# The first unit of the first branch's gates, computed between the mLSTM's heads

## The chip, the core and the metric

The kernel runs on one core of a Trainium2 chip. A core has TensorE (PE in the rows; the loading of its stationary operand is PEld), VectorE (DVE), ScalarE (ACT), GpSimd (POOL), and SyncE (SP), which issues nearly all of the weight loads. The metric is the time of one execution on the device in microseconds, and lower is better. A run's number is the median of several executions.

## What is computed

Two blocks follow each other over 256 tokens of 1024 features. The first has two layers with three branches each (an mLSTM, an attention over selected keys, and a differential attention), whose outputs are gated and summed. The second has a retention layer, a convolution and a mixture of eight experts. The change is in the first block, where each layer does this:

```python
def _layer(x, li, ...):
    z = jnp.einsum('btd,dc->btc', _rms(x, norm_mix_g), w_in)
    ...
    h = _mlstm(mq, mk, m_v, m_if[..., :M_HEADS], m_if[..., M_HEADS:])
    y_a = sigmoid(m_o) * _rms(h, m_norm_g)            # branch 0
    y_b = _dsa(sq, sk, sv, iq, ik, i_w)               # branch 1
    y_c = _rms(_diff_attn(dq, dk, dv, lam_val), ...)  # branch 2
    gates = jax.nn.sigmoid(g_pre + b_gate)            # g_pre: 3 x 1024 columns of z
    merged = (gates[:, :, 0] * (y_a @ w_branch[0]) + gates[:, :, 1] * (y_b @ w_branch[1])
              + gates[:, :, 2] * (y_c @ w_branch[2]))
    x = x + merged @ w_out
    ...

def _mlstm(q, k, v, i_pre, f_pre):
    ...
    sw = jnp.exp(dmat - m_t[..., None]) * jnp.einsum('bhntk,bhnsk->bhnts', qc, kc)
    num = jnp.einsum('bhnts,bhnsv->bhntv', sw, vc) + ...
```

## The kernel before

All engines' programs are written out by hand. Each engine runs its instructions in the order in which they are written and waits on semaphores. Nothing is scheduled for it.

**Products in two parts.** A large product is made of three matmuls, high x high, low x high and high x low (`mm3`). For each megabyte of weights (a *unit*) ACT therefore copies a rounded high part out of the ring of six load buffers (`column_highs`, 128x2048), and DVE then subtracts it to make the low part in place (`column_lows`). PE takes a unit only once its low part exists (`take_column` waits for `column_low`). The high part of each unit has a place of its own in memory, listed in `COLUMNS`. Those that matter here: unit g00 (first half of the first 512 gate columns of branch 0) goes to place H, b10 and b11 (the two units of branch 1's weights) go to A2 and D, g01 to E. Place D lies over the columns of z that hold the differential attention's queries and keys. It is free once PE has transposed them, which the kernel says with `place_free["D"]` behind `turn_heads`.

**Order on PE at the place of the change, once in each of the two layers.** The last products of branch 1's attention (`xs,pT`), then `mlstm_weights`: four transposes of the row vectors, then for each of the four heads an *exponents* product, which spreads a row over 128 partitions (its stationary operand has 4 rows, `ybuf,const`), and a *weights* product of queries and keys (`qkbuf`). DVE adds a mask to the exponents, ACT takes their exp, and DVE multiplies it with the weights product (L2413). Then `turn_branch` transposes branch 1's output (8 transposes, `const,yb`), and `turn_heads` the differential queries and keys (16, `const,z`). Then comes g00: 2 matmuls for the bias and 8 x 3 matmuls of 512 columns. Then `mlstm_values` (24 instructions of 129 columns, `v_ext,pbuf`), and `split_branch(1)`, which takes b10 and b11 both before its first matmul (48 matmuls of 512 columns, `ybuf_tmp_high`). The other three units of the gates follow.

**Order on ACT and DVE there.** ACT: exps of the four heads, two copies of branch 1's transposes, four copies of the heads' transposes, the high parts of b11, g01, g02, g03. DVE: the exponents' and weights' evacuations, the two low parts of branch 1, the low parts of b10 and b11, then `mlstm_values`' normalisation, the low part of g01, and the four merges of branch 1.

PSUM has eight banks, handed out in turn by `fill(ALL)`. It skips banks in `open_banks`, which g00's two banks are from its first matmul until g01 is done.

## Time and profile before

| | us |
|---|---|
| median of 3 executions | 2481.36 |
| lowest and highest | 2478.94, 2481.89 |
| span of the profiled execution | 2479.3 |
| PE busy in it | 2449.2 (99%) |
| DVE busy | 1850.2 (75%) |
| ACT busy | 1552.6 (63%) |
| mean granted TensorE clock | 0.994 of full |

The span runs from the first to the last instruction of one execution that the hardware profiler recorded. PE's busy time counts a matmul until its modelled end, so it covers gaps between starts. For the rate of PE, look at the starts of the weight loads (PEld) instead. The place of the change begins at 170.37 us in layer 0 and at 643.50 us in layer 1.

### The profile page before, as it was taken

The numbers are of one execution on the slowest core, as the hardware profiler recorded it, in microseconds if no ns is written. First come the engines' busy times: TensorE is split into PE (matmuls) and PEld (weight loads), VectorE is DVE, ScalarE is ACT, GpSimd is POOL, SyncE is SP. The second block draws the span as 40 slices with busy tenths as digits, with TensorE's granted clock in tenths as the row PEclk, the third lists the DMA queues.
The fourth block names the chain that finished last, engine by engine and source line by source line (L and its number), as shares of the span: only waits on it lengthen the run. The fifth ranks groups of instructions, "written<-read, shape, count | busy, mean of one in ns | idle before, by whom it ended". The sixth has DMA issues, their size and how long they took to land.

```text
span 2479.3 us, 30443 instructions
## 1 busy us (share of the span) xinstructions
PE 2449.2 (99%) x12028; PEld 2044.3 (82%) x12028; DVE 1850.2 (75%) x1856; ACT 1552.6 (63%) x1892; POOL 29.8 (1%) x36
## 2 busy tenths in 40 slices
PE   8999999999999999999999999999999999999998
PEld 8788888897887889978888997888888888788886
DVE  6877744478776546645545578999999999999998
ACT  5675543457565444365444447788878787878886
POOL 0000000000000000010000000000000000000001
PEclk9999999999999999999999998999999999999999
DMA  7444655354435565675555556999999999999996
GB/s 251 152 136 153 221 182 175 132 175 158 135 137 205 202 212 170 207 252 192 198 203 179 162 195 268 392 364 401 376 394 374 398 380 388 390 374 394 372 391 252
DMA packets 183223, 637.96 MB, mean 257 GB/s; under 512 B 11196, under 2 KB 52594, under 8 KB 139914
## 3 DMA queue, kind: packets, MB, share of 16 engines
q1 hardware_dynamic: 179562, 622.87, 68.3%
q0 software_dynamic: 3488, 12.59, 1.3%
q8 instruction: 132, 2.16, 0.3%
q14 instruction: 41, 0.34, 0.0%
HBM read 616.54 MB, written 18.88 MB: 256 GB/s over the span
## 4 chain that ended last, share of the span: by engine, by line
PE 92%; DVE 3%; DMA 2%; ACT 1%; issue 1%; SPq 0%; DVEq 0%; ACTq 0%
PE bank L561 88%; DVE split L2142 2%; PE bank L598 2%; PE bank L903 1%; DMA ring<-in_moe_w_gate 1%; DMA ring<-in_moe_w_up 1%; ACT split L1529 1%; ACT parts L1529 0%; DVE parts L2211 0%; PE bank L1449 0%; DVE oT_high L2156 0%; DVE parts L2122 0%; DMA const<-in_tables 0%; DVE x_resid L2184 0%; DVE tmp L2199 0%
## 5 line engine op out<-in xcount | busy, mean ns | idle before, releaser
L561 PE MATMUL bank<-split,parts 128*128 128x512 f32 (+1 forms) x6432 | 1467.4, 388 | 6.2 <-DVE parts L2211 1.8
L561 PEld LDWEIGHTS bank<-split,parts 128*128 128x128 f32 x6432 | 1186.6, 188 | 253.6 <-issue 15.2
L1529 ACT ACTIVATE split<-ring 128x2048 fp32r<-128x2048 f32 x444 | 848.7, 1922 | 441.6 <-PE bank L561 411.9
L2142 DVE TENSOR_TENSOR split<-ring,split 128x2048 fp32r<-128x2048 f32 x444 | 994.0, 2283 | 59.8 <-ACT split L1529 59.4
L2211 DVE TENSOR_TENSOR parts<-bank,parts 128x512 fp32r<-128x512 f32 x128 | 82.4, 686 | 159.0 <-ACT parts L1529 157.5
L1529 ACT ACTIVATE halves<-ring 128x1024 fp32r<-128x1024 f32 x96 | 101.0, 1061 | 129.9 <-PE bank L561 129.4
L2156 DVE TENSOR_TENSOR halves<-ring,halves 128x1024 fp32r<-128x1024 f32 x96 | 116.1, 1224 | 73.0 <-ACT halves L1529 72.3
L561 PE MATMUL bank<-ring_low,z_high 128*128 128x512 f32 (+2 forms) x384 | 146.9, 382 | 0.0
L561 PE MATMUL bank<-xparts,halves 128*128 128x256 f32 x960 | 116.4, 283 | 0.0
L561 PEld LDWEIGHTS bank<-xparts,halves 128*128 128x128 f32 x960 | 115.5, 192 | 0.5 <-DVE xparts L2122 0.2
L561 PE MATMUL bank<-z_high 128*128 128x512 f32 (+3 forms) x304 | 111.0, 365 | 0.0
L2201 DVE SCALAR_TENSOR_TENSOR tmp<-bank,xsum,tmp 128x512 f32<-128x512 f32 (+1 forms) x38 | 27.4, 722 | 109.4 <-PE bank L561 109.4
L1529 ACT ACTIVATE z_high<-ring 128x2048 fp32r<-128x2048 f32 (+2 forms) x42 | 77.4, 1867 | 46.0 <-PE bank L561 37.3
L1529 ACT ACTIVATE parts<-bank 128x512 fp32r<-128x512 f32 x160 | 86.0, 588 | 31.1 <-PE bank L903 15.5
L2358 DVE TENSOR_TENSOR ring_low<-ring,z_high 128x2048 fp32r<-128x2048 f32 (+2 forms) x42 | 93.3, 2239 | 12.8 <-ACT z_high L1529 12.4
L561 PE MATMUL bank<-z_high,oT_high 128*128 128x512 f32 (+2 forms) x240 | 92.3, 385 | 0.0
L561 PE MATMUL bank<-halves,xparts 128*128 128x512 f32 x384 | 89.2, 392 | 0.1
L561 PEld LDWEIGHTS bank<-halves,xparts 128*128 128x128 f32 x384 | 71.7, 188 | 15.5 <-issue 0.5
L561 PEld LDWEIGHTS bank<-ring_low,z_high 128*128 128x128 f32 x384 | 72.1, 188 | 12.1
L561 PE MATMUL bank<-split,oT_high 128*128 128x512 f32 x288 | 71.3, 397 | 0.5 <-DVE split L2142 0.5
L2199 DVE TENSOR_TENSOR tmp<-bank,tmp 128x512 f32<-128x512 f32 x112 | 71.7, 681 | 0.0
L1529 ACT ACTIVATE tmp<-bank 128x512 f32<-128x512 f32 x124 | 67.3, 593 | 6.5 <-PE bank L561 6.3
(342 smaller groups left out, 2335.2 us busy)
## 6 DMA issues: line engine op xcount, KB each, us to landing
ring<-in_moe_w_gate SPq DMA_DIRECT2D x112, 1024.0 KB, 8.2
ring<-in_moe_w_up SPq DMA_DIRECT2D x112, 1024.0 KB, 7.7
ring<-in_moe_w_down SPq DMA_DIRECT2D x112, 1024.0 KB, 7.8
ring<-in_w_gate_up SPq DMA_DIRECT2D x44, 1024.0 KB, 5.9
ring<-in_w_in SPq DMA_DIRECT2D x40, 1024.0 KB, 5.2
ring<-in_ret_w_in SPq DMA_DIRECT2D x24, 1024.0 KB, 5.3
ring<-in_w_down SPq DMA_DIRECT2D x22, 1024.0 KB, 7.0
ring<-in_w_in SPq DMA_DIRECT2D x20, 880.0 KB, 4.8
```

Of the source, the lines that this page charges most:

```text
L561: return nc.tensor.matmul(o, l, r, start=first, stop=final, **kw)
L598: ins = nc.tensor.transpose(bank[b][:, i * P:i * P + rows], src_of(i), ident[0:rows, 0:rows])
L903: return [nc.tensor.transpose(bank[b[tt]][:, f * P:(f + 1) * P], hb[:, tt, f * P:(f + 1) * P], ident) for f in range(n // P)]
L1529: return nc.scalar.activation(out, in_, func, **kw)
L2142: V.tensor_tensor(split[:, split_place(m), 1, :], ring[:, n % RING, :], split[:, split_place(m), 0, :].bitcast(F32), ALU.subtract).then_in ...
L2156: V.tensor_tensor(low, half_of(n, j, by_column), high.bitcast(F32), ALU.subtract).then_inc(half_low.sem, half_low.tick())
L2199: ins = V.tensor_tensor(hb[:, tt, 0:n], b[:, 0:n], sg[:, tt, 0:n], ALU.mult)
L2201: ins = V.scalar_tensor_tensor(hb[:, tt, 0:n], b[:, 0:n], xsum[:, 3, tt:tt + 1], sg[:, tt, 0:n], ALU.mult, ALU.mult)
L2211: V.tensor_tensor(low, b[:, 0:n].rearrange("p (f t) -> p f t", t=P), high.bitcast(F32), ALU.subtract).then_inc(hidden_low.sem, 1)
L2358: V.tensor_tensor(low, whole, column_place(named, k, width).bitcast(F32), ALU.subtract).then_inc(column_low.sem, column_low.tick())
```

## The change

`mlstm_weights` on PE becomes a generator that pauses after the exponents of heads 0 and 1 and after each head's weights product. `split_chunk` and `gate_tiles` take such a generator as `between` and advance it after every second k of each token tile, which is after every 6 matmuls. The first unit of branch 0's gates, g00, now runs with the heads inside it, and in front of both groups of transposes. Behind the transposes `mlstm_values` follows at once. No instruction is added or removed. The programs of ACT, DVE, POOL and SP are not edited.

```diff
-            def split_chunk(n, chunk, bias=None):
+            def split_chunk(n, chunk, bias=None, between=None):
...
                                            k == 0 and bias is None, k == KT - 1))
+                            if between is not None and k % 2 == 1:
+                                next(between, None)
...
-                mlstm_weights()
+                heads = mlstm_weights()
+                next(heads)
+                first_gates = gate_tiles(0, heads)
+                next(first_gates)
+                for _ in heads:
+                    pass
                 eng.wait_ge(dve_freed.sem, pe.point("dsa", dve_freed))
                 turn_branch(True)
                 turn_heads(lambda tt, c: zc(tt, C_DQ + c, P), lambda tt, c: zc(tt, C_DK + c, P))
                 place_free["D"] = [(for_act, for_act.marked)]
-                first_gates = gate_tiles(0)
-                next(first_gates)
                 mlstm_values()
                 split_branch(1)
...
                 exponents(0)
+                exponents(1)
+                yield
                 for h in range(4):
-                    if h < 3:
-                        exponents(h + 1)
                     b = fill(ALL)
...
                     point("weights")
+                    if h < 2:
+                        exponents(h + 2)
+                    yield
```

On PE, at the heads, before. The names are tiles: `ybuf,const` is an exponents product, `qkbuf` a weights product of 256 and 128 columns, `const,yb` a transpose of branch 1's output.

```order
L1277 MATMUL bank<-const,ybuf 128x4 x3
L561 MATMUL bank<-ybuf,const 128x256 [waits act_emptied,mqk_silu]
L561 MATMUL bank<-ybuf,const 128x256 [waits act_emptied]
L561 MATMUL bank<-qkbuf 128x256 [waits act_emptied]
L561 MATMUL bank<-qkbuf 128x128
L561 MATMUL bank<-ybuf,const 128x256 [waits act_emptied]
L561 MATMUL bank<-qkbuf 128x256 [waits dve_emptied]
L561 MATMUL bank<-qkbuf 128x128
```

And after, with the first matmuls of g00 (`bias_parts,bias_row`, `heads_high,z_high`, `ring_low,z_high`, `heads_high,oT_high`):

```order
L561 MATMUL bank<-ybuf,const 128x256 [waits act_emptied,mqk_silu]
L561 MATMUL bank<-ybuf,const 128x256 [waits act_emptied]
L561 MATMUL bank<-bias_parts,bias_row 128x512 [waits act_emptied]
L561 MATMUL bank<-bias_parts,bias_row 128x512
L561 MATMUL bank<-heads_high,z_high 128x512 [waits column_unit_low]
L561 MATMUL bank<-ring_low,z_high 128x512
L561 MATMUL bank<-heads_high,oT_high 128x512
L561 MATMUL bank<-heads_high,z_high 128x512
L561 MATMUL bank<-ring_low,z_high 128x512
L561 MATMUL bank<-heads_high,oT_high 128x512
L561 MATMUL bank<-qkbuf 128x256 [waits dve_emptied]
L561 MATMUL bank<-qkbuf 128x128
```

The bias and six matmuls of g00 stand ahead of head 0's weights product, and six more behind the products of heads 0, 1 and 2 each. The heads' own order is unchanged.

On PE, from the end of the heads' transposes (`const,z`) to branch 1's product, before (`v_ext,pbuf` is mlstm_values, `z_high,ybuf_tmp_high` the first matmul with b10):

```order
L598 MATMUL bank<-const,z 128x128 x3
L561 MATMUL bank<-bias_parts,bias_row 128x512 [waits dve_emptied]
L561 MATMUL bank<-bias_parts,bias_row 128x512
L561 MATMUL bank<-heads_high,z_high 128x512 [waits column_unit_low]
...
L561 MATMUL bank<-heads_high,oT_high 128x512
L561 MATMUL bank<-v_ext,pbuf 128x129 [waits act_emptied,inputs_low,dve_emptied]
L561 MATMUL bank<-v_ext,pbuf 128x129 x2
...
L561 MATMUL bank<-z_high,ybuf_tmp_high 128x512 [waits column_unit_low,act_emptied,inputs_low]
```

And after:

```order
L598 MATMUL bank<-const,z 128x128 [waits dve_emptied]
L598 MATMUL bank<-const,z 128x128 x3
L561 MATMUL bank<-v_ext,pbuf 128x129 [waits act_emptied,inputs_low,dve_emptied]
L561 MATMUL bank<-v_ext,pbuf 128x129 x2
...
L561 MATMUL bank<-z_high,ybuf_tmp_high 128x512 [waits column_unit_low,act_emptied,inputs_low]
```

The 26 matmuls of g00 no longer stand between the transposes and branch 1's product. Only the 24 instructions of `mlstm_values` do.

On ACT the rows keep their order. These stand behind the heads' exps, before and after alike (`ybuf_tmp_high` branch 1's copies, `qkbuf` the heads' copies, then the high parts of b11 and g01):

```order
L1529 ACTIVATE ybuf_tmp_high<-bank 128x512 [waits bank_for_act] x2
L1529 ACTIVATE qkbuf<-bank 128x512 [waits bank_for_act] x4
L1529 ACTIVATE z_high<-ring 128x2x1024 [waits bank_for_act,weights_loaded3]
L1529 ACTIVATE z_high<-ring 128x2x1024 [waits bank_for_act,weights_loaded4]
```

The high part of b11 still stands behind the heads' four copies and waits for PE's transposes. Nothing on ACT moved.

## Rows read from the trace of the kernel before

**Rows 1.** The profile's page: its span and the chain that ended last, by engine.
```profile
span 2479.3 us, 30443 instructions
PE 92%; DVE 3%; DMA 2%; ACT 1%; issue 1%; SPq 0%; DVEq 0%; ACTq 0%
```

**Rows 2.** Timeline of layer 1, PE: start, length, engine, line, tiles, count, [idle <-releaser].
```profile
643.50 0.32 PEld L1277 LDWEIGHTS bank<-const,ybuf 4*128 4x128 f32 x4
...
644.81 0.73 PEld L561 LDWEIGHTS bank<-qkbuf 128*128 128x128 f32 x4 [0.33 <-issue]
...
649.06 0.91 PEld L598 LDWEIGHTS bank<-const,yb 128*128 128x128 f32 x8
...
651.68 0.30 PEld L561 LDWEIGHTS bank<-bias_parts,bias_row 128*128 128x128 f32 x2
651.71 0.71 PE L561 MATMUL bank<-bias_parts,bias_row 128*128 128x512 f32 x2
...
657.60 2.88 PEld L561 LDWEIGHTS bank<-v_ext,pbuf 128*128 128x128 f32 x24
...
660.40 0.19 PEld L561 LDWEIGHTS bank<-z_high,ybuf_tmp_high 128*128 128x128 f32 x1
```

**Rows 3.** Timeline of layer 0, PE, the same three points of the program.
```profile
170.37 0.32 PEld L1277 LDWEIGHTS bank<-const,ybuf 4*128 4x128 f32 x4
...
181.81 0.30 PEld L561 LDWEIGHTS bank<-bias_parts,bias_row 128*128 128x128 f32 x2
...
190.46 0.19 PEld L561 LDWEIGHTS bank<-z_high,ybuf_tmp_high 128*128 128x128 f32 x1
```

**Rows 4.** Busy time by window: PE, PEld, DVE, ACT, POOL, then PEclk, DMA share, GB/s.
```profile
170.00:172.00 2.00, 2.00 (x13) 1.52 (x13) 1.42 (x5) 1.98 (x2) 0.00 (x0) 1.00 0.90 349
172.00:174.00 2.00, 2.00 (x9) 1.36 (x8) 1.11 (x4) 1.97 (x6) 0.00 (x0) 0.85 0.00 0
174.00:176.00 2.00, 2.00 (x6) 1.13 (x5) 1.27 (x4) 0.80 (x2) 0.00 (x0) 0.50 0.00 0
...
180.00:182.00 2.00, 2.00 (x19) 2.00 (x18) 1.73 (x3) 1.75 (x5) 0.00 (x0) 0.94 0.00 0
```

**Rows 5.** The same view in layer 1, over the same part of the program.
```profile
646.00:648.00 2.00, 2.00 (x9) 1.21 (x8) 1.47 (x5) 1.47 (x5) 0.00 (x0) 1.00 0.00 0
```

**Rows 6.** Timeline of layer 1, DVE and ACT, from g00's low part to b11's.
```profile
636.18 2.28 DVE L2358 TENSOR_TENSOR ring_low<-ring,heads_high 128x2048 fp32r<-128x2048 f32 x1
...
649.54 0.56 DVE L2413 SCALAR_TENSOR_TENSOR pbuf<-bank,pbuf 128x384 f32<-128x384 f32 x1 [0.27 <-ACT pbuf L1529]
...
650.44 1.29 DVE L2613 TENSOR_TENSOR ybuf_tmp_high<-bank,ybuf_tmp_high 128x512 fp32r<-128x512 f32 x2 [0.34 <-ACT ybuf_tmp_high L1529]
650.78 2.08 ACT L1529 ACTIVATE qkbuf<-bank 128x512 f32<-128x512 f32 x4
...
652.69 3.76 ACT L1529 ACTIVATE z_high<-ring 128x2048 fp32r<-128x2048 f32 x2
...
654.68 2.29 DVE L2358 TENSOR_TENSOR ring_low<-ring,z_high 128x2048 fp32r<-128x2048 f32 x1 [0.76 <-ACT z_high L1529]
```

**Rows 7.** Timeline of layer 0, DVE: b11's low part, and where DVE later catches up.
```profile
184.72 2.29 DVE L2358 TENSOR_TENSOR ring_low<-ring,z_high 128x2048 fp32r<-128x2048 f32 x1 [0.87 <-ACT z_high L1529]
...
199.11 0.69 DVE L2595 TENSOR_TENSOR xs<-bank,z 128x512 f32<-128x512 f32 x1 [1.82 <-PE bank L561]
```

**Rows 8.** Windows around two other gaps of PE: the router, and the start of layer 1's FFN.
```profile
1488.00:1490.00 2.00, 0.98 (x9) 0.78 (x8) 1.88 (x5) 1.77 (x6) 0.00 (x0) 1.00 0.02 4
1490.00:1492.00 2.00, 2.00 (x15) 2.00 (x15) 2.00 (x2) 1.80 (x6) 0.00 (x0) 0.74 0.00 0
...
768.00:770.00 2.00, 1.34 (x6) 0.75 (x4) 1.51 (x4) 2.00 (x7) 0.00 (x0) 1.00 1.04 384
```

**Rows 9.** Timeline of layer 1, PE: the longest gap that the layer's later part has.
```profile
770.26 3.01 PE L561 MATMUL bank<-split,parts 128*128 128x512 f32 x12 [0.91 <-DVE parts L2122]
```

More of the change, by code:

```diff
@@ L1065, in columns, with gate_tiles @@
                     point(name)
-                def gate_tiles(branch):
+                def gate_tiles(branch, between=None):
                     for i in range(2):
-                        yield from split_chunk(512, f"g{branch}", bias=6 * li + 2 * branch + i)
+                        yield from split_chunk(512, f"g{branch}", bias=6 * li + 2 * branch + i, between=between)
                     point("gates")
```

## The prediction, made before the run

> **What bounds the kernel now.** I read the page first, for its chain of waits: PE makes up 92% of it [rows 1]. So the time changes by what PE gains or loses, and a busy ACT or DVE matters only where PE waits for it. Next I read the timeline at the place of the change in both layers, and went by the starts of the weight loads, since PE's busy time hides gaps. Then came the granted clock by windows, because the two layers run the same instructions there and differ.
>
> In layer 1 the stretch from the first transpose of the row vectors to the first bias matmul of g00 takes 651.68 - 643.50 = 8.18 us [rows 2]. In layer 0 it takes 181.81 - 170.37 = 11.44 us [rows 3]. The 3.26 us between them are the clock: it is granted in full at 170 us, falls to 0.50 (1.2 GHz) inside the window from 172 us and is back during the one from 180 us [rows 4], while layer 1 keeps 1.00 (2.4 GHz) over the same instructions [rows 5]. Before that fall PE did only small products, with no gap that the trace puts down to another engine. In neither layer does PE wait there for ACT or DVE. What interrupts it is 0.33 us of "issue", three times, each where a 128-row stationary operand follows the 4-row one of an exponents product; the first of them is in the row at 644.81 [rows 2].
>
> **The change, part by part.** I measure each layer from the first row transpose, T, to the first matmul of branch 1's product. Before, that is 660.40 - 643.50 = 16.90 us in layer 1 [rows 2] and 190.46 - 170.37 = 20.09 us in layer 0 [rows 3].
>
> *The work on PE.* Nothing is added or dropped, so at full clock everything that used to run up to the start of mlstm_values still takes 657.60 - 643.50 = 14.10 us [rows 2]. The three 0.33 us gaps stay: an exponents product is still followed three times by a 128-row operand, now one of g00. What may be added is the switch from the heads' products back to the 512-column matmuls, made four times instead of once. The two bias matmuls take 0.71 us together [rows 2]. The 26 of g00 fill 657.60 - 651.68 = 5.92 us, 0.23 each, so a switch costs at most about 0.1. Three more give 0 to 0.3, and I take 0.3, since the row shows the switch itself. T to the start of mlstm_values is then 14.4 us.
>
> *What g00 needs earlier.* Its matmuls now start about 1.3 us behind T. Its low part is made at 636.18 + 2.28 = 638.46 us, 5 us ahead of T [rows 6]. It costs nothing, and were it late, it would cost the difference.
>
> *The heads' results.* mlstm_values needs the fourth head's weights from DVE, which come 1.0 us behind the start of branch 1's transposes (649.54 + 0.56 against 649.06) [rows 2, 6]. It now starts 2.6 us behind that point, as the 24 transposes stand between. Its first two banks are those of branch 1's transposes, and DVE frees both by 651.73, 2.7 us behind it [rows 6]. PE asks for the second 0.7 us later than the first, so neither is late. Cost 0, with about 0.6 us to spare at the banks.
>
> *The wait that appears.* b11's high part goes to place D and waits for the heads' transposes. ACT starts it at 652.69, behind its four copies, and DVE ends the low part at 654.68 + 2.29 = 656.97 [rows 6]. That is 5.29 us behind the end of the transposes (651.68) in layer 1, and 187.01 - 181.81 = 5.20 us in layer 0 [rows 3, 7]. Before, g00 (5.92 us) and mlstm_values (660.40 - 657.60 = 2.80 us) covered it with 3.4 us to spare. After, only the 2.80 us of mlstm_values do. Branch 1's product takes both units before it starts, so PE stands still for 5.3 + 0.05 - 2.8 = 2.55 us, once per layer. The 0.05 us are my allowance for the semaphore. The high part of b11 cannot come earlier: its place is read by the very transposes that moved back. No engine speeds up, since ACT and DVE idle ahead of it already (0.76 us on DVE) [rows 6].
>
> *Who is queued behind.* On DVE mlstm_values' normalisation stands behind b11's low part and begins at about 663 us instead of 661 us in layer 1's count. g01's low part follows it, but PE asks for g01 only 11 us later, after the 48 matmuls of branch 1. DVE has 1.82 us of idle ahead of a merge [rows 7], so it has caught up by the third merge. On SP the ring buffer of g00 is free about 3 us earlier, and a load that is not awaited starts earlier. The rest of the layer is shifted and nothing else.
>
> *The sum by layer.* T to branch 1's product is 14.4 + 2.8 + 2.55 = 19.75 us in both, if the clock stays up. Layer 0: 19.75 - 20.09 = -0.34. Layer 1: 19.75 - 16.90 = +2.85. Together +2.5 us, and the span goes from 2479.3 [rows 1] to 2481.8. The gain in layer 0 is the 3.26 us of the fallen clock: six 512-column matmuls now stand between the small products, so I expect no fall there.
>
> *The clock at the new gap.* Now the transposes, mlstm_values and a gap of 2.55 us stand in a row, 7.9 us from the first transpose of branch 1. The trace has gaps of both kinds: at the router the clock fell behind a window with about 1.0 us without PE work [rows 8], and at the FFN's start 0.66 us idle in a window and a gap of 0.91 us left it at 1.00 [rows 8, 9]. Mine is longer than either, so a fall is as likely as not in each layer. The price: the means of the two edge windows, 0.85 and 0.94, put layer 0's fall from 173.4 to 180.2 us, 6.8 us long [rows 4]. Over 512-column matmuls, that would be half of it, 3.4. Dense work follows here at once, so I take half, 1.7, and keep 0 and 3.4 as ends. One fall in the two layers: 2481.8 + 1.7 = 2483.5.
> The Trainium skill (TensorE: Matmul & The Clock Gate, the section on HAM oscillation) speaks against the change here: it says that a TensorE left idle is throttled back to half rate, and that what comes behind a wait for data starts cold. By this rule both layers would fall, and the sum would be 2481.8 + 2 x 1.7 = 2485.2. The trace agrees at the router, and at the FFN's start it shows a gap without a fall.
>
> *The scale.* The sum is made on a span of 2479.3, and the shown runs go from 2478.94 to 2481.89, median 2481.36, 2.1 above the span. The distance between the runs is about one fall of the clock. The change takes away such falls at the heads and puts others in at the gap, so I do not add the 2.1 to the sum; it is in the range.
>
> **Rivals.**
> *The clock holds in both layers.* Only the waits count: 2481.8. For it: the heads' stretch held in layer 1. Against: the new gap is the longest of the layer.
> *The gap does not appear.* Then only layer 0's 3.26 us come back, and the switches cost 0.6: 2479.3 - 3.3 + 0.6 = 2476.6. It needs b11's low part within 2.8 us of the last transpose, where the copy and the subtraction alone take 1.9 and 2.29 us (half of ACT's pair of 3.76, and DVE's row) [rows 6]. So this one is nearly excluded. It would not be outside 0.2% either.
> *The delay is taken up later.* PE waits 0.91 us for DVE at 770 us [rows 9]. But DVE's work there follows PE's own, and moves with it. It would take up under 1 us: about 2480.8.
> *Slower.* The mechanism is the clock at the new gap, in both layers. If each fall lasts as long as layer 0's did, 6.8 us, over branch 1's 512-column matmuls, each costs 3.4: 2481.8 + 6.8 = 2488.6, 0.3% to 0.4% slower. It decides from about 2.2 us per layer on, as 2481.8 + 4.5 is the bound. For it: PE does small products for 5 us ahead of the gap. Against: the work behind the gap is the densest that the layer has.
>
> **The numbers.** Forecast, the gap in both layers with one fall of the clock: 0.45, 2483.5. Clock holds: 0.28, 2481.8. Delay taken up: 0.08, 2480.8. No gap: 0.04, 2476.6. Slower: 0.15, 2488.6. A measurement of this kernel can tell about 0.2%, 5 us, from no change. The first three cases are inside it, and so is most of the fourth. The range has to hold 8 in 10. It starts at 2480.0, below the case of a delay taken up, and ends at 2487.5, which takes in two falls at 1.7 (2485.2) and the 2.1 us of the scale. Faster 0.04, same 0.82, slower 0.14.
>
> **What would show it.** (1) In the profile after, the heads' stretch has clock 1.00 in both layers, and mlstm_values starts 14.1 to 14.5 us behind T. (2) PE idles 2.3 to 2.8 us ahead of the first matmul of branch 1 (`z_high,ybuf_tmp_high`), released by DVE's low part of b11. (3) That low part ends 5.2 to 5.4 us behind the last transpose of the heads. (4) The clock by windows in the 7 us behind that gap says whether a fall was paid. (5) From the merges of branch 1 on, every row of a layer is shifted by one constant. I am wrong if PE waits inside the heads for DVE or ACT, if b11's low part is not what ends the gap, or if something later in the layer is late by more than the shift.

## The result, and the profile after

The changed kernel takes 2483.74 us (median of 21 executions, 2481.71 to 2485.55). The kernel before took 2479.72 us on the same chip (21 executions, 2476.62 to 2483.80). The ratio is 1.0016, with a 95% interval from 1.0010 to 1.0023. The change costs about 4 us. The forecast was 2483.5 us.

The profiled execution took 2484.42 us, with a span of 2482.6 against 2479.3 before. The page, span and chain that ended last, answers [rows 1]:

```profile
span 2482.6 us, 30443 instructions
PE 93%; DVE 3%; ACT 2%; DMA 2%; issue 1%; SPq 0%; DVEq 0%; ACTq 0%
```

The timeline of layer 1 in the changed kernel answers [rows 2] and [rows 6]. Columns are start, length, engine, line, operation, tiles, count, and the idle time with its releaser:

```profile
645.35 0.32 PEld L1282 LDWEIGHTS bank<-const,ybuf 4*128 4x128 f32 x4
...
646.66 0.30 PEld L561 LDWEIGHTS bank<-bias_parts,bias_row 128*128 128x128 f32 x2 [0.33 <-issue]
...
656.93 0.91 PEld L598 LDWEIGHTS bank<-const,yb 128*128 128x128 f32 x8
...
657.24 0.56 DVE L2421 SCALAR_TENSOR_TENSOR pbuf<-bank,pbuf 128x384 f32<-128x384 f32 x1 [1.49 <-PE bank L561]
...
658.65 2.08 ACT L1537 ACTIVATE qkbuf<-bank 128x512 f32<-128x512 f32 x4
...
659.55 2.76 PEld L561 LDWEIGHTS bank<-v_ext,pbuf 128*128 128x128 f32 x24
...
660.56 3.75 ACT L1537 ACTIVATE z_high<-ring 128x2048 fp32r<-128x2048 f32 x2
...
662.55 2.29 DVE L2366 TENSOR_TENSOR ring_low<-ring,z_high 128x2048 fp32r<-128x2048 f32 x1 [0.76 <-ACT z_high L1537]
...
665.07 0.19 PEld L561 LDWEIGHTS bank<-z_high,ybuf_tmp_high 128*128 128x128 f32 x1 [2.75 <-issue]
...
665.10 0.47 PE L561 MATMUL bank<-z_high,ybuf_tmp_high 128*128 128x512 f32 x1 [2.59 <-DVE ring_low L2366]
```

The transposes (8 of `const,yb`, then 16 of the heads) run right up to mlstm_values at 659.55. PE then stands still for 2.59 us in front of branch 1's product, and what releases it is DVE's low part of b11, which ends at 662.55 + 2.29 = 664.84. The gap is the same in layer 0, where the timeline has these rows beside [rows 3]:

```profile
169.38 0.32 PEld L1282 LDWEIGHTS bank<-const,ybuf 4*128 4x128 f32 x4
...
185.18 2.76 PEld L561 LDWEIGHTS bank<-v_ext,pbuf 128*128 128x128 f32 x24
...
190.68 0.19 PEld L561 LDWEIGHTS bank<-z_high,ybuf_tmp_high 128*128 128x128 f32 x1 [2.75 <-issue]
```

The windows show the clock (columns as in [rows 4]: PE, PEld, DVE, ACT, POOL, then PEclk, DMA share, GB/s). The first three are the heads of layer 0, the next four lie around the gap of layer 0, and the last three behind the gap of layer 1:

```profile
170.00:172.00 2.00, 2.00 (x9) 1.37 (x8) 1.42 (x6) 1.97 (x5) 0.00 (x0) 0.86 0.32 123
172.00:174.00 2.00, 2.00 (x6) 1.63 (x5) 0.00 (x0) 1.00 (x4) 0.00 (x0) 0.50 0.00 0
174.00:176.00 2.00, 2.00 (x8) 1.30 (x8) 0.83 (x2) 0.00 (x0) 0.00 (x0) 0.79 0.00 0
...
188.00:190.00 2.00, 0.13 (x2) 0.00 (x0) 1.83 (x1) 1.93 (x2) 0.00 (x0) 1.00 0.00 0
190.00:192.00 2.00, 1.29 (x6) 1.11 (x7) 1.86 (x11) 0.00 (x0) 0.00 (x0) 0.98 0.00 0
192.00:194.00 2.00, 2.00 (x6) 1.58 (x5) 2.00 (x8) 0.00 (x0) 0.00 (x0) 0.50 0.00 0
194.00:196.00 2.00, 2.00 (x7) 1.55 (x6) 2.00 (x2) 0.00 (x0) 0.00 (x0) 0.67 0.00 0
...
666.00:668.00 2.00, 2.00 (x8) 1.54 (x7) 2.00 (x9) 0.00 (x0) 0.00 (x0) 0.59 0.03 8
668.00:670.00 2.00, 2.00 (x7) 1.59 (x6) 2.00 (x1) 0.00 (x0) 0.00 (x0) 0.55 0.00 0
670.00:672.00 2.00, 2.00 (x10) 1.66 (x9) 0.75 (x2) 0.00 (x0) 0.00 (x0) 1.00 0.00 0
```

Behind both gaps the clock is at its lower level (0.50, 1.2 GHz) for about 3.4 us. In layer 0 it also fell over the heads, from about 171.4 to 174.8 us, in spite of g00's matmuls between them.

To see where the time went, I follow four marks: the first row transpose T of layer 0, the first turn of the residual (`x_resid`) in each layer, the router's first matmul and the first matmul of the experts (`split,parts`). These are the rows after, and before behind them for the last three:

```profile
298.71 1.09 PE L598 MATMUL bank<-const,x_resid 128*128 128x128 f32 x8 [0.26 <-DVE x_resid L2192]
...
773.11 1.09 PE L598 MATMUL bank<-const,x_resid 128*128 128x128 f32 x8 [0.26 <-DVE x_resid L2192]
...
1496.18 4.20 PE L561 MATMUL bank<-w_rt,xnT 128*128 128x8 f32 x32 [1.02 <-ACT xnT L1537]
...
1512.01 2.33 PE L561 MATMUL bank<-split,parts 128*128 128x512 f32 x9 [0.21 <-issue]
```

```profile
766.86 1.09 PE L598 MATMUL bank<-const,x_resid 128*128 128x128 f32 x8 [0.26 <-DVE x_resid L2184]
...
1489.93 6.04 PE L561 MATMUL bank<-w_rt,xnT 128*128 128x8 f32 x32 [1.02 <-ACT xnT L1529]
...
1508.57 3.70 PE L561 MATMUL bank<-split,parts 128*128 128x512 f32 x15
```

Before, layer 0's turn stands at 296.90. So T of layer 0 is 1.0 us earlier by itself, layer 0 is 2.8 us longer, and layer 1 is 4.4 us longer: +6.25 us, which stay unchanged down to the router. There 2.8 us come back: from the router's first matmul to the experts' first it takes 15.83 us instead of 18.64, and the router's own matmuls take 4.20 us instead of 6.04 (the rows above). The work is the same, and what differs is the granted clock. It falls there in both kernels. These are windows of the changed kernel, and behind them the one of the kernel before in which its clock is back (its fall begins in the window from 1490 us of [rows 8]):

```profile
1498.00:1500.00 2.00, 2.00 (x16) 2.00 (x17) 0.74 (x6) 1.46 (x3) 0.00 (x0) 0.81 0.39 86
...
1508.00:1510.00 2.00, 2.00 (x14) 2.00 (x13) 1.04 (x4) 0.60 (x1) 0.73 (x1) 0.63 0.04 8
```

```profile
1508.00:1510.00 2.00, 2.00 (x13) 1.78 (x13) 1.21 (x2) 1.48 (x3) 1.40 (x2) 0.99 0.94 371
```

By the means of these edge windows the clock is at half from 1499.2 to 1509.5 us after, 10.2 us, and from 1491.0 to 1508.0 us before, 17.1 us. What is left, 3.4 us at the experts, is what the span shows.

### The profile page after: what moved, and what is told of

Read it like the earlier page. It is cut to its first block, busy times and chain, and to the rows that moved or that the text cites. A ratio compares the mean times of both kernels' runs of the same rounds, so it can differ in the third digit from the quotient of the medians.

```text
span 2482.6 us, 30443 instructions
## 1 busy us (share of the span) xinstructions
PE 2447.2 (99%) x12028; PEld 2041.5 (82%) x12028; DVE 1850.1 (75%) x1856; ACT 1551.7 (63%) x1892; POOL 31.1 (1%) x36
## 4 chain that ended last, share of the span: by engine, by line
PE 93%; DVE 3%; ACT 2%; DMA 2%; issue 1%; SPq 0%; DVEq 0%; ACTq 0%
PE bank L561 89%; DMA ring<-in_moe_w_up 2%; PE bank L905 2%; PE bank L598 1%; DVE split L2150 1%; ACT split L1537 1%; ACT parts L1537 0%; DVE parts L2219 0%; PE bank L1457 0%; DVE ring_low L2366 0%; DVE oT_high L2164 0%; ACT ybuf_tmp_high L1537 0%; ACT z_high L1537 0%; DVE parts L2130 0%; DMA const<-in_tables 0%
## 5 line engine op out<-in xcount | busy, mean ns | idle before, releaser
L1537 ACT ACTIVATE parts<-bank 128x512 fp32r<-128x512 f32 x160 | 85.9, 588 | 28.0 <-PE bank L905 15.7
L2366 DVE TENSOR_TENSOR ring_low<-ring,z_high 128x2048 fp32r<-128x2048 f32 (+2 forms) x42 | 92.7, 2227 | 12.6 <-ACT z_high L1537 12.3
```

Of the source, the lines that this page charges most:

```text
L1537: return nc.scalar.activation(out, in_, func, **kw)
L2366: V.tensor_tensor(low, whole, column_place(named, k, width).bitcast(F32), ALU.subtract).then_inc(column_low.sem, column_low.tick())
```

## The experiments

**The theory.** The change has three effects on PE: (a) a gap of 2.6 us in front of branch 1's product, made by place D, once per layer; (b) a fall of the clock behind that gap; (c) milder or rarer falls over the heads, since 512-column matmuls stand among the small products. The rivals: the delay is taken up later and the gap costs nothing; the clock falls behind the gap whatever PE did in it; the interleaving is worth nothing and the difference between layers is chance; the time comes from something that the move shifts by the way, such as the rotation of the PSUM banks.

In the table, "T to values" and "T to b1" are the distances from the first row transpose to mlstm_values and to branch 1's first matmul, by the weight loads, in layer 0 and layer 1. Each ratio is to the kernel before on the same chip. The experiments are in four groups by chip: r_after and e1 to e3; e4 to e7; e8, e9, e10; e11. "Lost to the clock" is (1 - mean granted clock) x span, averaged over all executions of a run and not only the profiled one. The clock of an execution is recorded to 0.001, which is 2.5 us, so differences of less than about 1 us say nothing in this column.

| run | T to values | T to b1 | fell behind gap | median us | ratio, 95% | lost to the clock, us |
|---|---|---|---|---|---|---|
| before | 17.29, 14.10 | 20.09, 16.90 | no gap | 2479.72 | 1 | 13.0 to 13.7 |
| changed | 15.80, 14.20 | 21.30, 19.72 | both | 2483.74 | 1.0016 (1.0010 to 1.0023) | 12.6 |
| changed, again | 14.21, 14.20 | 19.72, 19.71 | both | 2484.81 | 1.0020 (1.0010 to 1.0029) | 12.4 |
| e1 | 15.80, 15.76 | 18.48, 18.44 | no gap | 2474.83 | 0.9979 (0.9970 to 0.9988) | 8.3 |
| e2 | 17.34, 17.39 | 22.85, 22.90 | both | 2493.15 | 1.0049 (1.0036 to 1.0063) | 18.4 |
| e3 | 14.21, 15.77 | 21.72, 23.28 | none | 2488.45 | 1.0034 (1.0022 to 1.0046) | 8.7 |
| e4 | 17.29, 14.10 | 20.09, 16.90 | no gap | 2480.57 | 1.0006 (0.9997 to 1.0016) | 13.4 |
| e5 | 15.79, 15.77 | 21.31, 21.28 | none | 2482.42 | 1.0013 (1.0004 to 1.0022) | 8.6 |
| e6 | 15.77, 14.17 | 18.45, 16.85 | no gap | 2476.46 | 0.9982 (0.9973 to 0.9991) | 9.0 |
| e7 | 14.20, 14.21 | 16.88, 16.89 | no gap | 2476.29 | 0.9988 (0.9980 to 0.9997) | 8.5 |
| e8 | 17.38, 14.22 | 20.06, 16.89 | no gap | 2482.57 | 1.0010 (1.0000 to 1.0019) | 14.9 |
| e9 | 14.20, 14.20 | 16.88, 16.88 | no gap | 2474.54 | 0.9975 (0.9966 to 0.9983) | 7.9 |
| e10 | 12.35, 12.35 | 15.03, 15.03 | no gap | 2487.78 | 1.0034 (1.0021 to 1.0048) | 15.3 |
| e11 | 12.34, 12.34 | 15.02, 15.02 | no gap | 2475.96 | 0.9980 (0.9971 to 0.9989) | 8.3 |

The value of before in the last column is that of the four chips of the experiments (13.1, 13.0, 13.7, 13.1). "T to values" has three levels in the interleaved kernels and before: 14.1 to 14.2 without a fall over the heads, 15.8 with a short one (+1.6), and 17.3 to 17.4 with a long one (+3.2). e10 and e11 do part of g00 ahead of T, so their 12.35 stands for 14.2.

### The changed kernel again, on the chip of e1 to e3

> The changed kernel once more, beside the others on the same chip. Theory of the gap (PE waits for the low part of b11): PE idles 2.5 to 2.7 us ahead of branch 1's product in both layers, and the clock falls behind the gap in one layer at least; time 3 to 5 us above the kernel before. Rival (the loss is the interleaving, in the heads' stretch): the same time, but the gap explains less than half of it.

Measured: the gap is the same to 0.01 us. Over the heads the clock held in both layers this time, and it fell behind both gaps. So the fall over the heads comes in some executions and not in others, and the one behind the gap came in 4 of 4 stretches. This is the window behind layer 0's gap:

```profile
190.00:192.00 2.00, 2.00 (x6) 1.52 (x6) 1.93 (x9) 0.00 (x0) 0.00 (x0) 0.50 0.03 8
```

### e1: b11 taken later, so that the gap is gone

```diff
-                    w = [take_column((2, 1024), f"b{br}") for _ in range(2)]
+                    w = [take_column((2, 1024), f"b{br}")]
...
+                    if br == 1:
+                        for tt in range(TT):
+                            first[tt] = fill(ALL)
+                            part(first[tt], 0, tt, (0, 1))
+                    w.append(take_column((2, 1024), f"b{br}"))
```

`part` issues the matmuls of the k that it is given. 12 matmuls that need only b10 run first, into two open banks, and then PE takes b11.

> The changed kernel, but split_branch(1) takes b10 first and runs the 12 matmuls of k = 0, 1 of both token tiles (12 x 0.23 = 2.8 us) before it takes b11, so the wait for b11's low part is covered. Theory of the gap: no gap, T to the first matmul of branch 1 17.0 to 17.4 us at full clock, the clock does not fall behind it; 2 x 2.6 for the gaps and up to 2 x 1.6 for the falls, 5 to 8.5 us below the changed kernel, so 1 to 4 us below the kernel before. Rival (interleaving costs the time): within 1 us of the changed kernel. Rival (delay would have been taken up later): within 2 us of it.

Measured: 10.0 us below the changed kernel on the same chip and 5.2 us below the kernel before. The timeline of e1, layer 0, shows the mechanism:

```profile
185.24 2.76 PEld L561 LDWEIGHTS bank<-v_ext,pbuf 128*128 128x128 f32 x24
...
187.92 0.19 PEld L561 LDWEIGHTS bank<-z_high,ybuf_tmp_high 128*128 128x128 f32 x1
...
188.24 2.29 DVE L2381 TENSOR_TENSOR ring_low<-ring,z_high 128x2048 fp32r<-128x2048 f32 x1 [0.75 <-ACT z_high L1552]
```

Branch 1's product starts before b11's low part has even begun, and no idle time stands in front of it. The gap (2.75) and the fall behind it (1.6) in two layers make 8.7 us. The medians differ by 10.0, more than the 5 to 8.5 that was expected. Over all executions e1 loses 4.1 us less to the clock than the changed kernel beside it (8.3 against 12.4), which with the two gaps makes 9.6. The profiled execution of e1, with a fall over the heads in both layers, is the slowest of its eleven (2478.94 us).

### e2: the move alone, without the interleaving

```diff
-                heads = mlstm_weights()
-                next(heads)
-                first_gates = gate_tiles(0, heads)
-                next(first_gates)
-                for _ in heads:
+                for _ in mlstm_weights():
                     pass
+                first_gates = gate_tiles(0)
+                next(first_gates)
```

> The changed kernel without the interleaving: all heads first, then the whole of g00, then the transposes. Theory of the gap: the gap stays at 2.5 to 2.8 us in both layers and the time within 2 us of the changed kernel: 0.6 less for the switches, up to 3 more where the clock falls over the heads. Rival (the interleaving costs the time): back at the kernel before, 4 us lower.

Measured: 2493.15 us, above everything expected. The gap is the predicted one, and PE's clock falls behind it as in the changed kernel. But over the heads both layers had the long fall this time (17.34 and 17.39), and 1.1 us came between layer 1's turn and the router. These two rows are waits of PE in e2, in the stretches from 950 and from 1100 us (total us, times, longest):

```profile
PE bank L561 <- DVE x_resid L2190: 0.8, 1, 0.8
...
PE bank L561 <- DVE parts L2128: 0.9, 1, 0.9
```

Only the first is new. The second is the 0.91 us of [rows 9], which in the kernel before and in the changed one stands at the start of layer 1's FFN and here comes in a later stretch. The remaining 0.3 us have no row. The same 0.8 us wait and the same 1.1 us stand in e3, e5 and e8, and in no other run. To the later products the fillers of e3 and e5 do nothing but take one turn of the PSUM banks in each layer, so the order in which banks come round is the likely cause. No run changes it alone here. In span e2 is 9.3 us above the changed kernel: 0.5 ahead of T, 1.6 and 3.2 over the heads, 1.1 in this stretch, 2.7 behind the router's start, and 0.2 elsewhere. It is one execution with two long falls. That a long fall in both layers is the rule for this order isn't shown by it. Its five executions lose 18.4 us to the clock on average, 6.0 more than the changed kernel beside it, so the others had falls of that size too.

### e3 and e5: fill the gap with idle work

```diff
                 mlstm_values()
+                filler(6, ALL)
                 split_branch(1)
```

e5 has `filler(3, ALL)`.

> The changed kernel with six products of the identity with a table (512 columns, result unused, about 0.43 us each) between mlstm_values and branch 1's product, so that PE works through the gap of 2.6 us. Theory that the gap lets the clock fall: clock 1.00 over branch 1's product in both layers, branch 1 starts where it did, 1.6 us per layer gained, up to 3.2 us below the changed kernel. Rival (the fall has another cause, or would come anyway): falls behind the gap as before and the time the same within 1 us.

> e3 with three idle products instead of six, since each took 0.79 us in e3's trace, not 0.43: 2.4 us of filling in a gap of 2.6. Theory that the gap makes the clock fall: branch 1 starts 5.5 us behind mlstm_values' start as in the changed kernel, the clock stays at 1.00 behind it in both layers, and the time is 2 to 3.2 us below the changed kernel, about 2482. Rival (filling costs elsewhere, or the falls stay): within 1 us of the changed kernel, or above.

Measured: a filler of 512 columns of plain fp32 takes 0.79 us in two instructions, so six of them took 4.75 us and overran the gap by 2.0 us in each layer. e3 is 3.6 us above the changed kernel. These 4.0 us and the 1.1 us named under e2, less the clock time won (8.7 against 12.4), make 1.4 of it, and the rest is open. The point of it stands: behind the fillers the clock did not fall, in either layer. e5 was made for the right size, and keeps the start of branch 1's product where the gap had put it (T to b1 less T to values is 5.5 us in both). Its timeline and a window behind the former gap, layer 0:

```profile
187.86 2.74 PE L561 MATMUL bank<-const 128*128 128x512 f32 x6
...
190.62 0.47 PE L561 MATMUL bank<-z_high,ybuf_tmp_high 128*128 128x512 f32 x1
...
192.00:194.00 2.00, 2.00 (x11) 1.60 (x10) 2.00 (x7) 0.00 (x0) 0.00 (x0) 1.00 0.00 0
```

The same wait without idleness leaves the clock at 1.00, where the changed kernel had 0.50 at 192 us. The idleness brings the fall, not the lateness of the product. The executions agree: e5 and e3 lose 8.6 and 8.7 us to the clock, the changed kernel 12.6 and 12.4. In time little of that arrives. Against the kernel before, e5 is 1.0013 where the changed kernel is 1.0016 and 1.0020: 0.7 to 1.7 us less, by ratios whose intervals overlap, where 2 to 3.2 us were expected. Of what is missing, 1.1 us are the new wait between layer 1's turn and the router.

### e4: b11 later in the kernel before

The edit is e1's, in the kernel before.

> The kernel before with split_branch(1) as in e1 (b10 first, b11 taken after 12 matmuls). There the low part of b11 is 3.4 us early, so nothing should be won. Theory (e1's gain is the gap that it closes, plus the cheaper falls of the clock over the heads): the kernel before, within 1.5 us. Rival (the new order inside split_branch is worth something of its own, and e1 owes its 5 us below the kernel before to that): 3 to 5 us below the kernel before.

Measured: 1.0006, not told from none. The marks equal those of the kernel before to 0.04 us all the way to 1508.56 us. So e1's gain is not in b11's order as such. It is there only where the move has opened the gap. The span of the profiled e4 is nevertheless 3.5 us lower than that of before, all of it behind 1508.56 us. The waits of PE there are, before:

```profile
PE bank L561 <- DVE parts L2211: 1.8, 2, 1.3
PE bank L561 <- issue: 1.7, 8, 0.3
PE bank L903 <- DVE tmp L2199: 1.1, 2, 0.7
PE bank L561 <- DVE split L2142: 0.9, 2, 0.5
```

and e4, the first two rows of the same view:

```profile
PE bank L561 <- issue: 1.3, 6, 0.3
PE bank L561 <- DVE split L2157: 0.9, 2, 0.5
```

The 2.9 us for `parts` and `tmp` come and go with the execution in the experts' stage, where the code is the same. In the two profiles of the changed kernel the wait for `parts` there is 3.4 and 0 us, the one for `tmp` 0 and 1.8 us. A single profile therefore can't decide about 3 us, and the verdicts here go by medians and by marks ahead of that stage.

### e6: e1, with branch 1's last gate unit later in the attention

```diff
-                    if j != 1 and j < 4:
+                    if j in (0, 2, 4):
                         next(between)
...
-                    if j == 4:
+                    if j == 5:
                         gate_tiles(1)
```

The first pair of lines is PE's program: the 24 matmuls of g13 come at step 4 of the loop instead of step 3. The second is ACT's, which takes their result one step later.

> e1, and branch 1's last gate unit (g13, 24 matmuls) one step later in the attention's loop on PE (j = 4 instead of 3, on ACT its sigmoids at j = 5), so that fewer small products stand in a row ahead of the heads. Theory that the clock falls over the heads because small products alone stand there for 4.7 us: no fall over the heads in either layer, start of mlstm_values 14.2 us behind T in both, 0 to 3.2 us below e1. Rival (the falls come anyway): as e1, 2475, with a fall in one or both layers.

Measured: 0.9982, e1's value within the interval. The theory fell. Over the heads the clock fell in layer 0 (15.77 us to the values) and held in layer 1, and over all executions e6 loses 9.0 us to the clock, e1 8.3. Fewer small products in a row ahead of the heads did not take the falls away, as the rival had it.

### e7: the gap closed where it arises

```diff
-            "g1": "E H A2 E", "b1": "A2 D", "g0": "H E A2 H", "g2": "A2 D E H", "b0": "G D", "b2": "H B"}
+            "g1": "E H A2 E", "b1": "A2 E", "g0": "H D A2 H", "g2": "A2 D E H", "b0": "G D", "b2": "H B"}
...
-                column_highs("b10")
+                column_highs("b10", "b11")
...
-                column_highs("b11", "g01", "g02", "g03")
+                column_highs("g01", "g02", "g03")
```

b11 goes to place E, which is free before the heads' transposes, and g01 takes D. DVE also makes b10's low part between the heads.

> The changed kernel with the wait taken away at its root instead: b11 goes to place E (free since g13) and g01 to D, ACT makes b11's high part ahead of the heads' exps, DVE makes b10's low part between the first two heads and b11's right behind branch 1's low parts. split_branch is untouched. Theory (the wait is for place D, the four copies and the two subtractions in a row): no gap, no fall behind it, the time as e1, 2474 to 2477. Rival (only the order of b10 and b11 in split_branch mattered, or ACT and DVE become late over the heads): a gap of 1 us or more stays, or a new one appears over the heads, 2478 or more.

Measured: no gap, no fall in either layer, T to b1 16.9 us, 2476.29 us (0.9988), 3.1 us below the kernel before. It shows the cause from the other side: with PE's program as in the changed kernel, the wait is gone once b11 is prepared ahead of the transposes. Three things changed together, the place, ACT's order and DVE's order, because the place is what allows the other two. How much each is worth alone was not run. The rows of the changed kernel give a measure: ACT starts b11's high part at 660.56 us, 1.01 us behind the end of the transposes, when its copies of them are done. With place D and no copies in front, an estimate from these rows is a gap of 2.59 - 1.01 = 1.6 us.

### e8 and e9: the interleaving, on one chip

e9 is e1 once more. e8 is e2 with e1's late b11, so the two differ only in whether g00's matmuls stand among the heads' products or behind them.

> e1 without the interleaving: all heads, then the whole of g00, then the transposes, and b11 taken late. Theory (interleaving is what shortens the falls of the clock over the heads, from 3.2 us each to 1.6 or none): no gap and no fall ahead of branch 1's product, but falls of 6.8 us over the heads, mlstm_values 17.3 us behind T; 3 to 5 us above e1, so at or a little above the kernel before. Rival (interleaving is worth nothing, e1 gains by the moved g00 and the late b11): as e1, within 1 us.

> e1 once more, as the measure for the two beside it on the same chip: 4 to 6 us below the kernel before.

Measured: 2482.57 against 2474.54, 8.0 us apart, where 3 to 5 were expected. In the profiles the spans are 7.1 us apart: 3.3 in layer 0's stretch, where e8 has the long fall and e9 none, 1.1 between layer 1's turn and the router (as in e2), 1.3 at the router, 0.9 in the experts, 0.5 elsewhere. These are windows of e8, layer 0:

```profile
172.00:174.00 2.00, 2.00 (x8) 1.40 (x7) 1.11 (x4) 1.96 (x6) 0.00 (x0) 0.76 0.00 0
...
176.00:178.00 2.00, 2.00 (x6) 1.73 (x7) 1.04 (x3) 0.80 (x2) 0.00 (x0) 0.50 0.00 0
178.00:180.00 2.00, 2.00 (x7) 1.63 (x7) 0.69 (x2) 0.00 (x0) 0.00 (x0) 0.53 0.00 0
```

Layer 1 had no fall in e8's profile (14.22 us to the values), against the expectation. Over all executions e8 loses 14.9 us to the clock and e9 7.9. These 7.0 us and the 1.1 us make 8.1, against the 8.0 measured, so the two account for the difference.

e9 repeats e1 on another chip: 0.9975 and 0.9979.

### e10 and e11: more of g00 ahead of the heads

e10 is e1 without `next(heads)`: the bias and the first six matmuls of g00 stand ahead of the row transposes. e11 is e10 with the banks handed out in e1's order:

```diff
-                heads = mlstm_weights()
+                at = turn[ALL]
+                turn[ALL] = at + 3
+
+                def heads_at():
+                    turn[ALL] = at
+                    yield from mlstm_weights()
+
+                heads = heads_at()
```

> e1 with g00's bias and first six matmuls ahead of the row transposes and the first exponents, instead of behind them: the small products behind branch 1's attention are then cut in two, 3.4 us and 1.3 us instead of 4.7. Theory (a fall needs the small products in one row): no fall over the heads in either layer, 0 to 3.2 us below e1. Rival (falls come by another rule than the length of this row): falls as in e1, and the time as e1.

> e10 with g00's two banks taken three turns further on, so that every bank of PSUM from the heads on is the one of e1. In e10 the second half of the gates was given a bank of the first half, and PE waited 4.2 us per layer for ACT's sigmoids (8.3 us in all). Theory (e10 lost by that bank alone, and the cut row of small products keeps the clock up over the heads): no wait for ACT, no fall over the heads in either layer, 0.994 to 0.998 of the kernel before, about 2473, and not above e1. Rival (putting gate matmuls first costs time in another way): 2476 or more, with a wait that e1 does not have.

Measured: over the heads the clock fell in neither run and in neither layer. But e10 is slow. T is 1.8 us later because 8 matmuls moved ahead of it (12.35 + 1.84 is 14.2, so nothing is lost there), and later PE waits twice for a bank that ACT still holds with the sigmoids of a gate. The timeline in layer 0, and the line in the waits of PE:

```profile
207.08 1.09 ACT L1551 ACTIVATE z<-bank 128x512 f32<-128x512 f32 x2
...
207.82 1.19 PE L561 MATMUL bank<-bias_parts,bias_row 128*128 128x512 f32 x2 [4.16 <-ACT z L1551]
...
PE bank L561 <- ACT z L1551: 8.3, 2, 4.2
```

The waits are not the whole cost. The clock falls in each of them, for 6.8 us. This is e10's window behind the end of the wait in layer 0:

```profile
208.00:210.00 2.00, 2.00 (x5) 1.61 (x6) 0.66 (x2) 0.17 (x1) 0.00 (x0) 0.50 0.06 24
```

From branch 1's first matmul to the residual's turn e10 takes 113.3 and 113.8 us in the two layers, e11 106.4 and 106.6. That is 14.1 us, of which 8.3 are the waits and the rest goes with the clock.

With the banks in e1's order (e11) the wait is gone, and with it 13 us by the two ratios, and the heads' windows stand at full clock, here layer 0 and layer 1:

```profile
166.00:176.00 10.00, 10.00 (x60) 8.11 (x59) 2.97 (x9) 5.98 (x9) 0.00 (x0) 1.00 0.31 105
...
640.00:650.00 10.00, 10.00 (x45) 7.27 (x44) 3.86 (x12) 4.68 (x11) 0.00 (x0) 1.00 0.06 24
```

The time, 0.9980, is e1's, and so is what it loses to the clock, 8.3 us. So the falls over the heads were rare enough in e1 already, or others came for them elsewhere; the runs don't tell which.

## Why the prediction was right

**The bound.** PE, as read from [rows 1]. It stayed so, and the time changed by what PE lost.

**The switches.** I added 0.3 us and said 14.4 us from T to mlstm_values. It is 14.20 where the clock held, against 14.10 before: 0.1 for three more switches. The row of 0.33 "issue" is there three times as before, and the return to 512 columns costs almost nothing.

**The heads' results, g00's low part and the banks.** Put at zero, and they cost zero. PE waits for nothing between T and the end of mlstm_values in either layer. DVE's last product of the heads (657.24 + 0.56 = 657.80) came 0.9 us behind the start of branch 1's transposes (656.93) in layer 1. The prediction had 1.0.

**The wait that appears.** b11's low part ends 664.84 - 659.55 = 5.29 us behind the end of the transposes; the prediction has 5.29. PE idles 2.59 us; it has 2.55. T to b1 is 19.72; it has 19.75. e1, e4 and e7 show that the late preparation of b11 is the cause: take the need away and 10 us go, do that without the gap and nothing goes, prepare b11 from another place ahead of the transposes and the gap is gone.

**The clock at the gap.** The price was right: 1.7 was expected for a fall, and it is 108.0 - 106.45 = 1.6 us, from the distance between branch 1's first matmul and the residual's turn with and without a fall, here layer 0 of the changed kernel against e1's. The count was wrong. I took one in two layers. It fell in 6 of 6 stretches with the bare gap (changed kernel, its repetition and e2), and in none of the 22 of the other kernels, where the gap was closed or filled or had never been. The Trainium skill (TensorE: Matmul & The Clock Gate, the section on HAM oscillation) describes this kind of fall, of a TensorE that waits for data and starts cold behind the wait, and the trace agrees, 6 of 6. But its example has waits longer than the 2.59 us here. The prediction applied it to this gap without saying so, and it is the six falls that decide. The gap of 0.91 us at the FFN's start in [rows 8, 9], which I had set against it, was no guide, and the length of a gap alone is none either: one of 1.02 us at the router is followed by a fall within 4 us in every profile.

**The clock over the heads.** "I expect no fall there" was too much. In layer 0 of the profiled execution mlstm_values starts 15.80 us behind T, outside the 14.1 to 14.5 that I had named as a sign. In the interleaved kernels (changed, repeated, e1, e3, e5, e6, e7, e9: 16 stretches) it fell in 7, and each lasted 3.4 us and cost 1.6. In the order that keeps the heads together (before, e4, e2, e8: 8 stretches) it fell in 5 (layer 0 in 4 of 4, layer 1 in 1 of 4), and each lasted 6.8 us and cost 3.2. Per stretch that is 0.7 against 2.0 us, or 2.6 us for both layers, where the sum had 3.3 on the one layer that happened to have a fall. That is the mean of a dozen profiled executions. All executions say more: beside each other on one chip, the kernel before loses 13.1 us to the clock and e1 8.3, and e8 loses 14.9 and e9 7.9. So the interleaving is worth about 5 to 7 us of clock time. How much of that lies at the heads and how much elsewhere, at the router above all, the means don't tell. That a fall over the heads is of half the length is in every row.

**The sum.** As predicted: -0.34 in layer 0, +2.85 in layer 1, +1.7 for one fall: +4.2 on the span. Measured in the profiles: +1.21 to branch 1's first matmul and +1.59 behind it in layer 0, +2.82 and +1.58 in layer 1, so +7.2, less 1.0 us by which T came earlier. The missed 3.0 are the 1.6 of the second fall behind a gap and the 1.6 of the fall over the heads in layer 0, less small terms. The profiled span is all the same only 3.3 us longer, as 2.8 us came back at the router, a term that no step of mine had. From the router's first matmul to the experts' first, the profiles of all kernels lie between 15.7 and 18.7 us, and those of one and the same kernel at 15.83 (changed) and 17.42 (repeated), so I can't put this down to the change. Over all executions the sum closes better: on the chip of r_after the changed kernel waits 5.2 us more at the two gaps and loses 0.7 us less to the clock than the kernel before (12.4 against 13.1), which makes +4.5. The medians differ by 4.8.

**What was luck.** The mechanism of the waits was right, but the number came out as close as it did by luck. The forecast let the clock give back 3.3 us at the heads and take 1.7 at the gap, 1.6 less in all. In the runs the interleaving gives back about 5 us and the two falls behind the gap take 3.2 to 4.1 (12.4 against 8.3 for e1), about 0.7 less in all. Both terms were too small, with opposite signs. The level was luck too. The sum stands on a span, and times are 1.8 us above spans in these runs. It met the time because the median before is 2479.72 over 21 executions, and not the 2481.36 of the first three.

**The scale.** "The distance between the runs is about one fall of the clock" is only part of it. Executions of one kernel are 3 to 12 us apart, and those with the higher mean clock are mostly the faster ones: on the chip of r_after the kernel before has a mean time of 2482.3 us at a clock of 0.993 and of 2477.6 at 0.996. In the profiles the DVE waits in the experts' stage differ by up to 2.9 us (before against e4) and the stretch at the router by 1.6 us (the changed kernel against its repetition). The falls over the heads alone don't make it.

**The rivals.** "Clock holds" (2481.8) fell with the 6 of 6. "No gap" (2476.6) fell with the row at 665.10, and it is e1, e7 and e9 that give what it describes, at 2474.5 to 2476.3. "Taken up later" fell: the +6.25 us are there unchanged from layer 1's turn to the router. The slower case had the mechanism right, with the falls at half the price it needed.

**A better version.** e1 (and e9), the interleaving with b11 taken later, is faster than both: 0.9979 and 0.9975 of the kernel before on two chips, about 10 us below the changed kernel. e11 gives the same, e7 (0.9988) a little less, by intervals that overlap.

## What to carry to other kernels

When a step is moved ahead of others, list what it used to cover behind them: here g00's 5.9 us hid the two-step preparation of a weight unit whose place in memory those very transposes read, and only 2.8 us of cover were left. A bare wait of 2.6 us on TensorE cost 4.2 us with the fall behind it, so begin such a product with the half that is ready, as e1 does, and spread small products among large ones where nothing waits on them.

## What the runs showed of the hardware

- The granted clock falls over the small products with no gap but the 0.33 us of "issue": 1.6 us lost with 512-column matmuls among them, 3.2 us when they stand alone, in 7 of 16 and in 5 of 8 stretches. The same code fell in one layer and held in the other.
- A gap of 2.59 us of PE was followed by a fall of about 3.4 us in 6 of 6 stretches. With idle products in it, three or six, it was followed by none in 4 of 4. In each of the two waits of 4.2 us in e10 it fell for 6.8 us.
- A product of 512 columns in plain fp32 takes 0.79 us in two instructions, against the 0.23 us of one high or low matmul of g00 at full clock (5.92 us for 26, [rows 2]).
- Which PSUM bank the next product gets can be worth more than the move itself: 8.3 us of waits and 13 us of time in e10, gone in e11. The 1.1 us in e2, e3, e5 and e8 go with the order of the banks as well, though no run shows that they come from it.
- The kernels lose from 7.9 (e9) to 18.4 us (e2) to the clock on average. Between kernels of one chip this makes 4.8 of the 5.2 us from before to e1, and 7.0 of the 8.0 us from e9 to e8.
